# Rotary halves swapped by transfers between SBUF partitions instead of a product with a matrix, in the attention layer and the odd layer

## The chip, the cores and the metric

The kernel runs on one core of a Trainium2 chip. The metric is the device time of one execution in microseconds (us). The core has TensorE for matmuls (PE in the rows, its weight loads PEld), VectorE (DVE), ScalarE (ACT), GpSimd (POOL) and SyncE (SP), and 16 DMA engines; transfers are issued here from the queues of SP and ACT.

## The reference, cut to what matters

Two networks run one behind the other on a sequence of 512 tokens of width 1024: pool, gated delta, latent attention and pool layers, then an even and an odd layer. Two of them rotate queries and keys by position.

```python
# latent attention ("mla"), 16 heads; the last 64 of 192 query channels are rotated, one rotated key for all heads
def rope(x, pos):
    half = x.shape[-1] // 2                      # 32
    inv = ROPE_THETA ** (-jnp.arange(half, dtype=jnp.float32) / half)
    ang = pos.astype(jnp.float32)[..., None, None] * inv
    cos, sin = jnp.cos(ang), jnp.sin(ang)
    x1, x2 = x[..., :half], x[..., half:]
    return jnp.concatenate([x1 * cos - x2 * sin, x1 * sin + x2 * cos], axis=-1).astype(x.dtype)

# odd layer: 8 heads with two maps of 64 channels each; the first 16 of 64 channels are rotated
def partial_rotary(t, pos):
    half = ROT_DIM // 2                          # 8
...
    t1, t2 = tf[..., :half], tf[..., half:ROT_DIM]
    out = jnp.concatenate([t1 * cos - t2 * sin, t2 * cos + t1 * sin, tf[..., ROT_DIM:]], axis=-1)
```

In the odd layer q and k are normalised over their 64 channels (RMS with a gain) before the rotation; in the attention layer the rotated parts are not normalised by themselves. Both layers then do a softmax attention, gate it and project it back onto x.

## The kernel before, in words

Activations lie transposed in SBUF: channels on the 128 partitions, the 512 tokens along the row. All semaphore waits are written out by hand, and each engine runs its own instruction stream in order.

**Weights.** They come from HBM in slots of up to 512 KB into a ring of four (`load_slot`, SP). ACT makes a rounded copy of a slot (`slot_hi`, L276), POOL the remainder in four pieces (`slot_lo`, L291), and `product` multiplies with three matmuls of 512 columns for each block of 128 x 128 (L310, L311, L312) into one of four PSUM banks, `gbank`. PE waits for the remainder and for the bank; the next tile of the bank waits until DVE or ACT has taken the last one. The other four banks, `wbank`, are for everything else.

**Attention layer (`mla_layer`).** A first part (`c_tensor`, `c_vector`, `c_scalar`) projects x onto the latent vectors and the rotary key: eleven slots with one tile each, the fifth the key. Then come 8 pairs of heads. Pair 0's projections run alone (`in_pieces`), and its rotary step after it. Each of seven turns then does, on PE: the attention of pair i (`work_tensor`) with the projections of pair i+1 between its steps, the rest of these, the rotary product (`prep_tensor`, L2325), the output products of pair i (`out_tensor`, two slots with four tiles each). The last pair has no projections beside it. ACT copies the rotary part of q from PSUM into `xr` (`evac_scalar`, L2314, the seventh tile), DVE takes the two gate tiles (`evac_gate`, L2320) and then does the rotary step in `prep_vector`: a product with the cosine (L2334), a product of the rotated tile in PSUM with the sine (L2336), their sum (L2338); then it adds the eight output tiles to x (L482). The next `work_tensor` waits for the sum.

**Odd layer (`odd_layer`).** DVE builds the tables (`tables_vector`, L2592), after it has waited for the norm's factor R; a small matmul of PE (L2616) waits for its step "lq lk", which comes after them. Then 4 pairs of heads in the same manner, with 3 turns. The rotary step has four tiles (two of k, two of q): ACT squares them (L2653), PE sums the squares (`prep_tensor_a`, L2640), ACT makes 1/rms by Ln and Exp (L2656, L2660), DVE multiplies (`prep_vector_a`, L2671), PE multiplies by the rotary matrix (`prep_tensor_b`, L2645), and DVE combines them (`prep_vector_b`, L2679, L2682, L2685). In a turn PE does the sums, one half of the output products (four tiles, `out_half`), the four rotary products, the other half, one projection of the next pair (slot 9), and then the transposes of v (L2695), ahead of which it waits for the last sum of the rotary step. DVE takes the first half's four tiles behind L2671 and one tile of the second half behind each rotary sum, and then the last gate tile (L2633). ACT converts the slots that become free (`hi_after`) between these steps.

**The rotary matrix** is float32, 128 x 128, and each product of 128 x 512 with it goes to the engine as two matmuls. It holds the swap of the halves and the sign.

```python
def prep_tensor(pe, s, i, h):                                                    # L2325
    tp.turn()
    pe.wait_ge(*tile_taken(s, i, *TILES[6]))
    pe.wait_ge(*ve.at("y 1", h, 1))
    pe.matmul(wbank(2), rot, xr, start=True, stop=True).then_inc(*tp.done("rotated"))
```

## Time and profile before

| | us |
|---|---|
| median of 3 runs | 2773.35 |
| lowest, highest | 2770.08, 2773.97 |
| profiled execution, its own time | 2769.89 |
| its span, first to last instruction | 2768.1 |
| mean granted clock of TensorE | 0.976 |

Busy shares of the span: PE 95%, PEld 74%, DVE 58%, POOL 41%, ACT 38%. A busy share is an average over stages; which engine sets the time in a stage is read from the chain of waits and the timelines. Times in a timeline are counted from the span's start. The attention layer runs from about 950 to 1590, the odd layer from about 2375 to the end.

### The profile page before, as it was taken

How to read it: one execution, taken by the hardware profiler on the slowest of the kernel's cores; microseconds unless marked ns; L12 is line 12 of the kernel's file. 1: busy time of each engine (PE TensorE's matmuls, PEld its weight loads, DVE VectorE, ACT ScalarE, POOL GpSimd, SP SyncE). 2: the span in 40 equal slices, each digit the busy share in tenths (PEclk: the TensorE clock that was granted, in tenths of full speed). 3: DMA queues.
4: the chain of work that ended last, by engine and by line, in shares of the span. 5: the costliest groups of instructions: out<-in, count | busy, mean ns of one | idle time of the engine just before them, and what ended most of it. 6: DMA issues, size and time to landing. Idle time of an engine off the chain costs nothing.

```text
span 2768.1 us, 32858 instructions
## 1 busy us (share of the span) xinstructions
PE 2621.5 (95%) x11934; PEld 2042.0 (74%) x11934; DVE 1599.7 (58%) x2703; ACT 1050.3 (38%) x1559; POOL 1141.2 (41%) x1446
## 2 busy tenths in 40 slices
PE   7999998999999898999999899998999998989996
PEld 6888777888888666777777688886887766756664
DVE  4654565777777523444333555556898953366565
ACT  3222343433343433233332422225445663445543
POOL 4666532333333342333333266654554424414320
PEclk9999999999999999999999999999999999999997
DMA  3332311122211221222221233222322212202110
GB/s 122 98 106 92 105 54 39 61 61 62 61 61 46 67 65 54 70 63 70 64 72 54 67 107 99 92 92 77 97 87 69 65 43 76 85 30 69 61 39 31
DMA packets 57106, 196.02 MB, mean 71 GB/s; under 512 B 6416, under 2 KB 8976, under 8 KB 56976
## 3 DMA queue, kind: packets, MB, share of 16 engines
q1 hardware_dynamic: 55824, 192.90, 22.3%
q8 instruction: 82, 1.34, 0.2%
q10 hardware_dynamic: 1152, 1.38, 0.2%
q14 instruction: 48, 0.39, 0.0%
HBM read 192.16 MB, written 2.10 MB: 70 GB/s over the span
## 4 chain that ended last, share of the span: by engine, by line
PE 85%; DVE 9%; ACT 3%; issue 2%; DMA 1%; SPq 0%; ACTq 0%; DVEq 0%
PE psum L310 23%; PE psum L312 22%; PE psum L311 22%; PE psum L1738 3%; PE psum L2393 1%; PE psum L2363 1%; DVE psum L884 1%; PE psum L423 1%; PE psum L1744 1%; PE psum L2366 1%; PE psum L2387 1%; PE psum L2706 1%; PE psum L2735 1%; PE psum L1130 1%; ACT whi L276 1%
## 5 line engine op out<-in xcount | busy, mean ns | idle before, releaser
L291 POOL TENSOR_TENSOR wlo<-raw,whi 128x256 fp32r<-128x256 f32 x1436 | 1140.7, 827 | 1564.9 <-ACT whi L276 1564.9
L310 PE MATMUL psum<-xh,whi 128*128 128x512 f32 x1832 | 763.9, 417 | 15.2 <-DVE xl L404 8.5
L312 PE MATMUL psum<-xh,wlo 128*128 128x512 f32 x1832 | 719.9, 393 | 0.0
L311 PE MATMUL psum<-xl,whi 128*128 128x512 f32 x1832 | 719.1, 393 | 0.0
L276 ACT ACTIVATE whi<-raw 128x1024 fp32r<-128x1024 f32 (+1 forms) x367 | 377.8, 1036 | 803.1 <-PE psum L312 803.1
L310 PEld LDWEIGHTS psum<-xh,whi 128*128 128x128 f32 x1832 | 347.4, 190 | 95.5 <-issue 29.2
L312 PEld LDWEIGHTS psum<-xh,wlo 128*128 128x128 f32 x1832 | 346.5, 189 | 76.2
L311 PEld LDWEIGHTS psum<-xl,whi 128*128 128x128 f32 x1832 | 347.8, 190 | 73.0 <-issue 9.7
L482 DVE TENSOR_TENSOR xT<-psum,xT 128x512 f32<-128x512 f32 x248 | 167.3, 687 | 206.0 <-PE psum L312 206.0
L310 PE MATMUL psum<-pool_yh,whi 128*128 128x512 f32 x256 | 102.5, 400 | 0.0
L311 PE MATMUL psum<-pool_yl,whi 128*128 128x512 f32 x256 | 101.7, 397 | 0.0
L312 PE MATMUL psum<-pool_yh,wlo 128*128 128x512 f32 x256 | 101.5, 396 | 0.0
L576 DVE TENSOR_TENSOR pool_u<-psum,R 128x512 f32<-128x512 f32 x32 | 22.1, 692 | 132.4 <-PE psum L312 132.3
L2323 DVE TENSOR_TENSOR mwork<-psum,R 128x512 f32<-128x512 f32 x16 | 11.1, 691 | 123.1 <-PE psum L312 123.1
L884 DVE SCALAR_TENSOR_TENSOR psum<-e_ue,par,psum 128x512 f32<-128x512 f32 x112 | 79.8, 744 | 0.0
L2435 DVE TENSOR_REDUCE mxs<-psum 128x1 f32<-128x128 f32 (+3 forms) x64 | 31.2, 487 | 77.2 <-PE psum L2368 77.2
L2404 ACT ACTIVATE mwork<-psum,nmx 128x128 f32<-128x128 f32 (+3 forms) x64 | 33.8, 528 | 98.5 <-DVE nmx L2437 98.5
L2318 ACT ACTIVATE mwork<-psum 128x512 f32<-128x512 f32 x48 | 27.6, 596 | 103.1 <-PE psum L312 91.9
L1690 DVE SCALAR_TENSOR_TENSOR g_qv<-pre,par,g_qv 128x512 f32<-128x512 f32 x72 | 64.7, 899 | 1.5
L310 PE MATMUL psum<-cqh,whi 128*128 128x512 f32 x144 | 61.1, 424 | 3.5 <-issue 3.5
L310 PE MATMUL psum<-gyh,whi 128*128 128x512 f32 x128 | 58.9, 460 | 4.4 <-DVE gyl L2022 4.4
L312 PE MATMUL psum<-cqh,wlo 128*128 128x512 f32 x144 | 57.7, 401 | 0.0
(524 smaller groups left out, 4515.4 us busy)
## 6 DMA issues: line engine op xcount, KB each, us to landing
raw<-weights_dram SPq DMA_DIRECT2D x335, 512.0 KB, 3.5
raw<-weights_dram SPq DMA_DIRECT2D x32, 384.0 KB, 3.0
xin<-x_dram SPq DMA_DIRECT2D x4, 512.0 KB, 7.0
out_dram<-y SPq DMA_DIRECT2D x4, 512.0 KB, 2.6
g_masks<-gdn_masks_dram ACTq DMA_DIRECT2D x1, 384.0 KB, 4.1
par<-params_dram SPq DMA_DIRECT2D x1, 326.5 KB, 3.4
mwork<-positions_dram ACTq DMA_DIRECT2D x1, 256.0 KB, 3.0
o_pT<-positions_dram ACTq DMA_DIRECT2D x1, 256.0 KB, 3.1
```

The lines of the kernel that those rows point to most:

```text
L276: act.activation(whi[:, q, 0:nk * nm * P], raw[:, q, 0:nk * nm * P], ACT.Copy).then_inc(hi_ready[q], 1)
L291: last = pool.tensor_tensor(wlo[:, q, part], raw[:, q, part], whi[:, q, part].bitcast(F32), ALU.subtract)
L310: pe.matmul(gbank(b), whi[:, q, c:c + P], h, start=k == 0, stop=False)
L311: pe.matmul(gbank(b), whi[:, q, c:c + P], l, start=False, stop=False)
L312: done = pe.matmul(gbank(b), wlo[:, q, c:c + P], h, start=False, stop=k == nk - 1)
L423: pe.matmul(wbank(0), ones, sq[:, k % 2, :], start=k == 0, stop=k == KD - 1).then_inc(*te.done(f"sum {k}"))
L482: dve.tensor_tensor(xT[:, t, :], tile(sec, j, m), xT[:, t, :], ALU.add).then_inc(*taken(sec, j, m))
L884: dve.scalar_tensor_tensor(out=out, in0=src[:, k:k + SEQ], scalar=w, in1=old, op0=ALU.mult, op1=ALU.add).then_inc(*ve.done(f"tap {c} {k}"))
L1690: dve.scalar_tensor_tensor(out=dst, in0=pre[:, x, k:k + SEQ], scalar=w, in1=dst, op0=ALU.mult, op1=ALU.add).then_inc(*ve.done(f"{i} tap {k ...
L1738: last = pe.matmul(wbank(b)[:, c * P:(c + 1) * P], left[:, c, :], right[:, c, :], start=True, stop=True)
L2404: act.activation(prob[:, hd, off_q[t]:off_q[t] + w], wbank(x % 4)[:, 0:w], ACT.Exp, scale=SCALE, bias=nmx[:, x:x + 1], accum_out=rs[:, x:x ...
L2435: dve.reduce_max(mxs[:, x:x + 1], wbank(x % 4)[:, 0:w], AX.X).then_inc(*ve.done(f"max raw {x}"))
```

## The change

A transfer can move rows to other partitions, so the swap of the halves is left to the DMA engines, and the sign goes into the sine table: the frequencies of the first half of each block are negated on the host, by which the sine changes its sign and the cosine doesn't. In the attention layer ACT issues four transfers of 32 partitions by 512 (64 KB each), for k and after each copy of the rotary part of q, into a new tile `xrot`. In the odd layer ACT issues four transfers of 8 partitions by 2 x 512 (32 KB each) for k once two tiles are normalised, and four for q once all are, into a new tile `rotb`. Its other rows stay zero, for which DVE clears it once, with one instruction at the head of the tables. DVE's sine product now reads these tiles and waits for 64 on the transfers' semaphore. The rotary products, their steps and the matrices are gone.

```diff
@@ attention layer @@
+            def rotate(act, x):
+
+                for r in (0, 64):
+                    act.dma_start(xrot[r:r + 32, :], x[r + 32:r + 64, :]).then_inc(rotated, 16)
+                    act.dma_start(xrot[r + 32:r + 64, :], x[r:r + 32, :]).then_inc(rotated, 16)
...
-                dve.wait_ge(*tb.at("k rotated"))
-                dve.tensor_tensor(krx, wbank(2), sinT[:, :], ALU.mult).then_inc(*vbs.done("k sin"))
+                dve.wait_ge(rotated, 64)
+                dve.tensor_tensor(krx, xrot[:, :], sinT[:, :], ALU.mult).then_inc(*vbs.done("k sin"))
...
                     if j == CKV:
+                        act.wait_ge(*tile_taken(c_sec, 0, CKV, 0))
+                        rotate(act, krx)
                         continue
...
-                    if j == CKV + 2:
-                        pe.wait_ge(*tile_taken(c_sec, 0, CKV, 0))
-                        pe.matmul(wbank(2), rot, krx, start=True, stop=True).then_inc(*tb.done("k rotated"))
...
                 act.activation(dst, tile(s, j, m), ACT.Copy).then_inc(*taken(s, j, m))
+                if t == 6:
+                    act.wait_ge(*tile_taken(s, i, j, m))
+                    rotate(act, xr)
...
-            def prep_tensor(pe, s, i, h):
-                tp.turn()
-                pe.wait_ge(*tile_taken(s, i, *TILES[6]))
-                pe.wait_ge(*ve.at("y 1", h, 1))
-                pe.matmul(wbank(2), rot, xr, start=True, stop=True).then_inc(*tp.done("rotated"))
...
-                dve.wait_ge(*tp.at("rotated", h))
-                dve.tensor_tensor(Rt[:, :], wbank(2), sinT[:, :], ALU.mult).then_inc(*vp.done("sin"))
+                dve.wait_ge(rotated, (h + 2) * 64)
+                dve.tensor_tensor(Rt[:, :], xrot[:, :], sinT[:, :], ALU.mult).then_inc(*vp.done("sin"))
...
@@ odd layer @@
+            rotb = sb("o_rotb", [P, 4, SEQ])
...
             def tables_vector(dve):
+                dve.memset(rotb[:, :, :], 0.0).then_inc(*vbs.done("rotated 0"))
                 dve.wait_ge(pos_in, 32)
...
-            def prep_tensor_b(pe, h):
-                for x in range(4):
-                    pe.wait_ge(*vp.at(f"normed {x}", h))
-                    pe.matmul(wbank(x), rot, xq[:, x, :], start=True, stop=True).then_inc(*tp.done(f"rotated {x}"))
...
                     act.activation(rr[:, x, :], rr[:, x, :], ACT.Exp, scale=-0.5).then_inc(*ap_.done(f"1/rms {x}"))
+                for q in range(2):
+                    act.wait_ge(*vp.at(f"normed {2 * q + 1}", h))
+                    rotate(act, q)
+
+            def rotate(act, q):
+
+                pair = slice(2 * q, 2 * q + 2)
+                for r in (0, 64):
+                    act.dma_start(rotb[r:r + 8, pair, :], xq[r + 8:r + 16, pair, :]).then_inc(rotated[q], 16)
+                    act.dma_start(rotb[r + 8:r + 16, pair, :], xq[r:r + 8, pair, :]).then_inc(rotated[q], 16)
...
-                    dve.wait_ge(*tp.at(f"rotated {x}", h))
+                    dve.wait_ge(rotated[x // 2], (h + 1) * 64)
                     dve.wait_ge(*vp.at(f"cos {x}", h))
-                    dve.tensor_tensor(xq[:, x, :], wbank(x), sinT[:, :], ALU.mult).then_inc(*vp.done(f"sin {x}"))
+                    dve.tensor_tensor(xq[:, x, :], rotb[:, x, :], sinT[:, :], ALU.mult).then_inc(*vp.done(f"sin {x}"))
...
-    out["mla_inv"] = (10000.0 ** (-(r % 32) / 32.0)).astype(np.float32).reshape(P, 1)
+    out["mla_inv"] = (np.where(r % 64 < 32, -1.0, 1.0) * 10000.0 ** (-(r % 32) / 32.0)).astype(np.float32).reshape(P, 1)
```

## Rows read from the trace of the kernel before

**Rows 1.** Page: the chain's shares by engine; one group of DVE.

```profile
PE 85%; DVE 9%; ACT 3%; issue 2%; DMA 1%; SPq 0%; ACTq 0%; DVEq 0%
...
L482 DVE TENSOR_TENSOR xT<-psum,xT 128x512 f32<-128x512 f32 x248 | 167.3, 687 | 206.0 <-PE psum L312 206.0
```

**Rows 2.** Rotary products by line: ns (min, median, max), first and last start.

```profile
L2329 PE MATMUL psum<-sq,mk x16: 590/590/591, 1076.3 to 1522.0; 128*128 128x512 f32 x16
...
L2299 PE MATMUL psum<-mwork,mk x2: 592/592/592, 1007.5 to 1007.9; 128*128 128x512 f32 x2
...
L2645 PE MATMUL psum<-o_xq,o_mk x32: 591/592/1177, 2431.3 to 2685.6; 128*128 128x512 f32 x32
```

**Rows 3.** Timeline, PE at a turn's end: start, length, [idle before <- releaser].

```profile
1521.32 0.39 PE L312 MATMUL psum<-xh,wlo 128*128 128x512 f32 x1
...
1521.55 1.02 PE L2329 MATMUL psum<-sq,mk 128*128 128x512 f32 x2
...
1522.64 0.39 PE L311 MATMUL psum<-myl,whi 128*128 128x512 f32 x1
```

**Rows 4.** The sine product and its addition in the attention layer, by line.

```profile
L2336 DVE TENSOR_TENSOR Rt<-psum,sinT x8: 682/684/685, 1077.7 to 1523.0; 128x512 f32<-128x512 f32 x8
...
L2338 DVE TENSOR_TENSOR mwork<-sq,Rt x8: 693/1212/1217, 1078.4 to 1523.7; 128x512 f32<-128x512 f32 x8
```

**Rows 5.** Timeline: ACT's copy of rotary q; PE behind the first call.

```profile
1510.83 0.60 ACT L2318 ACTIVATE sq<-psum 128x512 f32<-128x512 f32 x1 [2.66 <-PE psum L312]
...
1079.64 1.97 PE L2353 MATMUL psum<-cst,mwork 128*128 128x128 f32 x8 [2.35 <-DVE mwork L2338]
```

**Rows 6.** A memset by line; timelines of DVE and PE at the odd layer's start.

```profile
L569 DVE MEMSET pool_onesrow<- x2: 485/485/485, 38.1 to 1588.1; 128x512 f32 x2
...
2381.18 0.84 DVE L2594 CAST o_maskb<-cst 128x128 bf16<-128x128 f32 x1 [7.09 <-ACT R L440]
...
2386.69 0.38 PE L2616 MATMUL psum<-o_lam,cst 64*128 64x2 f32 x2 [3.48 <-DVE o_lam L2600]
```

**Rows 7.** Timeline of DVE and PE in the first rotary step of the odd layer.

```profile
2430.44 2.74 DVE L2671 SCALAR_TENSOR_TENSOR o_xq<-o_xq,par,o_rr 128x512 f32<-128x512 f32 x4 [8.21 <-ACT o_rr L2660]
...
2434.01 0.69 DVE L2682 TENSOR_TENSOR o_xq<-psum,o_sinT 128x512 f32<-128x512 f32 x1
...
2441.86 1.97 PE L2695 MATMUL psum<-cst,o_vT 128*128 128x128 f32 x8 [5.21 <-DVE o_qr L2685]
```

**Rows 8.** Timeline: an ACT issue. Two groups of issues (KB, us to landing).

```profile
2375.22 0.46 ACTq L2901 DMA_DIRECT2D o_mk<-odd_masks_dram  x1
...
pool_head<-pool_head_dram ACTq DMA_DIRECT2D x2, 32.0 KB, 1.9
...
xin<-x_dram SPq DMA_DIRECT2D x4, 512.0 KB, 7.0
```

**Rows 9.** Timelines of PE, DVE and POOL in the first odd turn.

```profile
2514.03 3.60 PE L2645 MATMUL psum<-o_xq,o_mk 128*128 128x512 f32 x8
...
2528.53 1.04 PE L2695 MATMUL psum<-cst,o_vT 128*128 128x128 f32 x8
...
2514.79 2.48 DVE L482 TENSOR_TENSOR xT<-psum,xT 128x512 f32<-128x512 f32 x4
...
2517.19 0.83 DVE L2679 TENSOR_TENSOR o_rr<-o_xq,o_cosT 128x512 f32<-128x512 f32 x1
...
2526.73 1.09 DVE L2685 TENSOR_TENSOR o_qr<-o_rr,o_xq 128x512 f32<-128x512 f32 x1
...
2515.37 3.25 POOL L291 TENSOR_TENSOR wlo<-raw,whi 128x256 fp32r<-128x256 f32 x4 [5.10 <-ACT whi L276]
```

**Rows 10.** Timeline: PE's sums, first odd turn; DVE's gate copy, third.

```profile
2504.91 3.70 PE L2640 MATMUL psum<-o_rr,o_mk 128*128 128x512 f32 x8 [1.67 <-ACT o_rr L2653]
...
2697.30 0.69 DVE L2633 TENSOR_TENSOR o_gs<-psum,R 128x512 f32<-128x512 f32 x1 [0.63 <-PE psum L312]
```

**Rows 11.** Stretch: us, busy time by engine, granted clock (PEclk), DMA share, GB/s.

```profile
2442.00:2446.00 4.00, 3.22 (x13) 2.49 (x14) 1.29 (x2) 0.00 (x0) 0.00 (x0) 0.50 0.00 0
```

More of the change, by code:

```diff
@@ L2173, in mla_layer @@
             kr = sb("kr", [P, SEQ])
-            mk = sb("mk", [P, 2, P])
-            rot = mk[:, 0, :]
+            mk = sb("mk", [P, P])
+            xrot = sb("mla_xrot", [P, SEQ])
             maskb = sb("maskb", [P, 2, P], BF16)
@@ L2217, in c_vector @@
                 dve.tensor_copy(identb, ident).then_inc(*vbs.done("identity"))
-                dve.tensor_copy(causal, mk[:, 1, :]).then_inc(*vbs.done("mask"))
+                dve.tensor_copy(causal, mk[:, :]).then_inc(*vbs.done("mask"))
                 rotary_tables(dve, None, vbs, ab, "vector", pos_i, cosT[:, :], sinT[:, :], tmp, param("mla_inv"),
@@ L2532, in tables @@
                 act.dma_start(pos_i, T["positions"].to_broadcast([P, SEQ])).then_inc(pos_in, 16)
-                act.dma_start(mk[:, :, :], T["mla_masks"].rearrange("p (k n) -> p k n", k=2)).then_inc(pos_in, 16)
+                act.dma_start(mk[:, :], T["mla_masks"]).then_inc(pos_in, 16)
             def sync(sp):
@@ L2558, in odd_layer @@
             sinT = sb("o_sinT", [P, SEQ])
-            mk = sb("o_mk", [P, 3, P])
-            rot, halves = mk[:, 0, :], mk[:, 2, :]
+            mk = sb("o_mk", [P, 2, P])
+            halves = mk[:, 1, :]
+            rotb = sb("o_rotb", [P, 4, SEQ])
             maskb = sb("o_maskb", [P, 2, P], BF16)
@@ L2580, in odd_layer @@
             tmp = [rr[:, 0, :], rr[:, 1, :], rr[:, 2, :]]
-            pos_in = sem("odd_pos_in")
+            pos_in, rotated = sem("odd_pos_in"), [sem(f"odd_rotated_{name}") for name in ("k", "q")]
             wq, wk, subln = param("c_q_norm_w"), param("c_k_norm_w"), param("c_subln_w")
@@ L2592, in tables_vector @@
             def tables_vector(dve):
+                dve.memset(rotb[:, :, :], 0.0).then_inc(*vbs.done("rotated 0"))
                 dve.wait_ge(pos_in, 32)
                 dve.tensor_copy(identb, ident).then_inc(*vbs.done("identity"))
-                dve.tensor_copy(allowed, mk[:, 1, :]).then_inc(*vbs.done("mask"))
+                dve.tensor_copy(allowed, mk[:, 0, :]).then_inc(*vbs.done("mask"))
                 rotary_tables(dve, None, vbs, ab, "vector", pos_i, cosT[:, :], sinT[:, :], tmp, param("odd_inv"),
@@ L3131, in small_parameters @@
     r = np.arange(P)
-    out["mla_inv"] = (10000.0 ** (-(r % 32) / 32.0)).astype(np.float32).reshape(P, 1)
+    out["mla_inv"] = (np.where(r % 64 < 32, -1.0, 1.0) * 10000.0 ** (-(r % 32) / 32.0)).astype(np.float32).reshape(P, 1)
     out["c_norm_w"] = columns(A["c_norm_w_2"][0])
-    out["odd_inv"] = np.where(r % 64 < 16, 500000.0 ** (-2.0 * (r % 8) / 16.0), 0.0).astype(np.float32).reshape(P, 1)
+    out["odd_inv"] = np.where(r % 64 < 16, np.where(r % 64 < 8, -1.0, 1.0) * 500000.0 ** (-2.0 * (r % 8) / 16.0),
+                              0.0).astype(np.float32).reshape(P, 1)
     for name in ("c_q_norm_w", "c_k_norm_w"):
@@ L3183, in constants @@
         c[f"join {s}"] = (p // (2 * s) == x // (2 * s)) & (p // s % 2 == 0) & (x // s % 2 == 1)
-    rot = np.zeros((P, P), np.float32)
-    for m in range(P):
-        if m % 64 < 32:
-            rot[m + 32, m] = -1.0
-        else:
-            rot[m - 32, m] = 1.0
-    orot = np.zeros((P, P), np.float32)
-    for m in range(P):
-        if m % 64 < 8:
-            orot[m + 8, m] = -1.0
-        elif m % 64 < 16:
-            orot[m - 8, m] = 1.0
     t = np.arange(SEQ)
     head = np.stack([w * (1.0 / np.minimum(t + 1, w)).astype(np.float32) for w in WINDOWS])[:, 0:PAD].astype(np.float32)
-    odd_masks = [orot, np.where((x >= 64) & (p < 64), NEG, 0.0), p // 64 == x // 64]
+    odd_masks = [np.where((x >= 64) & (p < 64), NEG, 0.0), p // 64 == x // 64]
     return {"odd_masks": np.concatenate([m.astype(np.float32) for m in odd_masks], axis=1),
-            "mla_masks": np.concatenate([rot, np.where(x > p, NEG, 0.0).astype(np.float32)], axis=1),
+            "mla_masks": np.where(x > p, NEG, 0.0).astype(np.float32),
             "consts": np.concatenate([c[k].astype(np.float32) for k in ("identity", "ones")], axis=1),
```

12 lines of the change are left out of this document (4 added, 8 removed).

## The prediction

> **What bounds the kernel now.** I read the chain of work that ended last first: 85% of it is TensorE (PE), 9% VectorE (DVE) [rows 1]. The costliest groups say the same from the other side: DVE's additions of a product to x sat idle 206 us, all of it waiting for a product of PE [rows 1]. So in a stretch where PE has no idle time, a PE instruction taken away is gained, and DVE work added there is free. The timelines of the two layers then show where this does not hold: the start of the odd layer, the first rotary step of each layer, and the end of each odd turn, where DVE is as long as PE.
>
> **What is removed from PE.** A rotary product is one call and two matmuls of 590 to 592 ns in the trace (their spans overlap; what counts is how much later the next one starts). There are 8 calls in the attention turns, 1 for k, 16 in the odd layer [rows 2].
> - Attention turns: at the end of a turn L312 starts at 1521.32, and after the rotary product L311 of the next product starts at 1522.64. Neighbours start 0.23 apart, so without it L311 would start at 1521.78: 0.86 us [rows 3]. PE is busy on both sides and then goes into eight output products, in which DVE waits. 7 of the 8 calls stand so: 7 x 0.86 = -6.0 us. What takes their place is hidden: ScalarE (ACT) copies the rotary part of q out at 1510.83 and DVE's sine product starts at 1523.0, 12 us later [rows 4, 5]; four transfers of 64 KB issued by ACT need some 4 us of it (below). ACT issues them ahead of a conversion of weights, which comes some 1.8 us later; PE needs that slot only after two more products of 24 matmuls at 0.23 (11 us), so nothing is late.
> - k: a product of the same length [rows 2] among the first projections, PE busy around it, and what follows (the norms of c, DVE's operands) hangs on PE's last product: -0.86 us. DVE asks for its swap only after four more projections of 24 matmuls, 22 us.
> - The first attention call: PE waits for DVE behind it (2.35 us idle [rows 5]), so its removal is worth 0.
> - The odd layer: below, since the gain there depends on DVE.
>
> **What the sine product costs DVE.** It read PSUM and now reads two SBUF tensors. In the attention turns the PSUM form took 682 to 685 ns every time, also beside GpSimd (POOL); the addition behind it, with two SBUF inputs, took 693 ns alone but 1212 at the median, that is 0.52 us more, and in the odd turn 1.09 [rows 4, 9]. I read this as DVE waiting for a running POOL instruction, between 0 and 0.52 us a time, and take 0.45 for each one that meets POOL. The Trainium skill has this as a rule that speaks against this change: in "SBUF — State Buffer", section "🔬 SBUF: two separate sides", a DVE instruction with two SBUF inputs and a GpSimd instruction exclude each other for a whole instruction. These rows agree with it for the addition; for the sine product no row of before shows it. A second rule of the Trainium skill, in "VectorE: DVE Perf Modes", section "⚠️ The TRN2 errata — SBUF-src ops pay a fixed extra latency per instruction", has a PSUM source cost 62 cycles more than an SBUF one, about 65 ns as an estimate, which would give back 0.26 us in an odd turn. The trace disagrees: the PSUM form is not the longer one (684 against 693 ns alone) [rows 4].
> - In attention turns this is covered: DVE has 0.7 us idle ahead of nearly every addition to x, and it catches up. In the first call DVE's chain is what PE waits for, one hit more: +0.5 (0 to 0.8).
>
> **The start of the odd layer.** DVE now clears four 512-column tiles, after its wait for R and ahead of the tables [rows 6]. A memset of 512 columns took 485 ns, so 4 x 0.485 = 1.94 us. PE already waits 3.48 us there, for DVE's lambda step, which comes after the tables; nothing covers the memset. The CAST at 2381.18 took 0.84 us beside POOL and may get shorter behind the memset, by less than its length. So +1.1 to +1.94; I take +1.5.
>
> **The first rotary step of the odd layer.** Here the chain is ACT, DVE, PE; POOL is idle. The four normed tiles start at 2430.44, two of them are done by 2431.9; the sine product started at 2434.01, and PE waited 5.21 us for the end of it [rows 7]. Afterwards ACT issues four transfers from 2431.9. An issue took 0.46 us, a transfer of 32 KB landed 1.9 us after its issue, the heaviest 7.0 [rows 8]. The fourth is issued at about 2433.3 and lands at about 2435.2: +1.4 us (0.5 to 3; SBUF to SBUF is in no row, the nearest is the small one of 32 KB). The second pair has 3 us more. PE's rotary products lay in its idle time: 0.
>
> **The three odd turns.** PE starts the rotary products at 2514.03; they hold it for 8 x 0.43 = 3.44 us, to 2517.47. Without them the next output half has to wait for a bank: the same four banks hold the first half, and DVE takes them only behind its normed tiles, from 2514.79, first done at 2515.48 [rows 9]. PE starts at 2515.5, so it is 2.0 us ahead, and would be ready for the transposes at 2526.55 in place of 2528.53. But those wait for the last rotary addition, which ends at 2527.8. So even with no cost at all only 0.7 of 3.44 us is left, and 0.5 behind it, since DVE must still copy the gate. Two normed tiles are done at 2513.6, so the swap lands by 2517.0, before the cosine product ends at 2518.0 [rows 9]: no wait there.
>
> Now the four sine products. Two batches of POOL (8 instructions) run in DVE's rotary stretch, the first at 2515.37 [rows 9]; eight issues of ACT push it to about 2518. DVE's cosine, sine and addition then all have two SBUF inputs, each waits for the one before, and POOL slips in between. Followed with 0.6 and 0.7 us a piece, sine products and additions meet POOL six times: 6 x 0.45 = 2.7, where before it was 0.15 for the first cosine product (0.83) and 0.40 for the last addition (1.09) [rows 9]. The last addition ends 2.15 us later, at 2529.95. PE is 1.4 us later than before, and it has been idle for 3.4 us. After an idle of 2.35 us the eight transposes took 1.97 us, against 1.04 in the turn, and behind the idle of 5.21 the granted clock was 0.50, the level of 1.2 GHz, for the 4 us from 2442 [rows 5, 7, 9, 11]. Transposes slower by 0.93 and a clock at half for some 5 us cost about 2.4 us. So +3.8 us each in the first two turns. In the third POOL has nothing to do, and the gate's copy, before which DVE was idle 0.63 us, is earlier by that: -0.6 [rows 10]. Together +7.0.
>
> **The sum.** -6.0 - 0.86 + 0.5 + 1.5 + 1.4 + 7.0 = +3.5 us. The profiled execution took 2769.89 us (span 2768.1), so it becomes 2773.4. That execution is the fastest of four (2769.89, 2770.08, 2773.35, 2773.97); their middle is 2771.7, the median of the runs 2773.35. I forecast 2775, the sum laid on the middle of the four, rounded. A measurement of this kernel can tell about 0.2%, 5.5 us, from no change.
>
> **The rivals.**
> - The sine products don't meet POOL (the form of the instruction matters less than I think). Then the first call costs 0, the turns give -0.5 - 0.5 - 0.6: -6.0 - 0.86 + 1.5 + 1.4 - 1.6 = -5.6, some 2766. For it: a cosine product with two SBUF inputs beside POOL is not always longer. Against it: the additions.
> - They meet POOL, but PE's clock holds over the idle of 3.4 us, or the idle is shorter: 3.5 - 4.8 = -1.3, some 2770.5. The rows of 2.35 and 5.21 us speak against it.
> - Slower than before: the transfers land late. A load of weights may be under way beside them, and their rows lie in few partitions. The place is the first sine product of each odd step. The first step has no reserve, so each us of landing beyond 1.9 costs one; in the turns the reserve is 1.0 us, from there each us costs one three times. At the landing of 7.0 us: first step +5 more, the turns 3 x 3.9, about a third of which falls together with waits for POOL: +3.5 + 5 + 8 = +16, some 2788. It decides from a landing of about 3.5 us. For it stands only the row of 7.0, of four transfers of 512 KB at once; against it the small ones.
> - The clock also falls after the bank wait of 1.45 us: 3 x 2.4 more, +10.7, some 2782. Against it: in the same turns PE is idle 1.67 us ahead of the sums of squares, and those eight matmuls then take no longer than 0.46 us each, 3.70 in all [rows 10].
>
> **How the numbers follow.** Forecast 0.42, no meeting 0.23, clock holds 0.17, late landing 0.08, clock at the bank wait 0.05, other 0.05. The range reaches from the first rival with its scatter to the forecast with the upper ends of its terms: 2765 to 2781. Faster by over 0.2%: half of the first rival and a little of the second, 0.15. Slower: a quarter of the forecast's cases, late landing and the clock, 0.22. Within: 0.63.
>
> **What would show it.** In the attention turns L311 follows L312 with no gap and each turn is 0.86 us shorter. In the odd turns PE shows a wait of about 1.4 us for DVE's addition to x, then one of 3 us for the last rotary addition, with transposes of 1.97 us in two turns of three; sine products of 1.1 to 1.2 us beside POOL. At the odd layer's start PE waits about 5 us for lambda. The sine product of the first odd step starts about 3.5 us behind the second normed tile. If the sine products stay at 0.68 us the term of 7.0 is wrong; if the transfers take over 3.5 us the sign of the whole is.

## The result, and the profile after

The kernel after took 2779.71 us at the median (2776.86 to 2781.78, 15 runs), the kernel before, timed beside it, 2774.39 us (2769.94 to 2777.51, 15 runs). The ratio is 1.0022, 95% interval 1.0015 to 1.0029: slower by some 5.3 us. The forecast was 2775, with a sum of +3.5 and a range of 2765 to 2781; I held a change within 0.2% for the likeliest, and the ratio lies just outside, with that bound inside its interval. The profiled execution of after took 2781.18 us, its span is 2779.4.

The page of after answers to [rows 1]: the chain of work that ended last, and DVE's additions to x.

```profile
PE 83%; DVE 10%; ACT 4%; issue 3%; DMA 1%; ACTq 0%; SPq 0%; DVEq 0%
...
L482 DVE TENSOR_TENSOR xT<-psum,xT 128x512 f32<-128x512 f32 x248 | 166.6, 687 | 197.8 <-PE psum L312 197.8
```

Two points of the chain's share went from PE to DVE, ACT and issue. To see where, I put the two traces side by side at the same instructions. The table has the times between two instructions in the one profiled execution of each kernel, in us.

| stretch | before | after | difference | in the sum |
|---|---|---|---|---|
| DVE's first CAST of the attention layer to the first transposes of a pair | 115.43 | 116.38 | +0.95 | -0.36 |
| to the transposes of the eighth pair (seven turns) | 453.96 | 447.82 | -6.14 | -6.0 |
| to lambda's matmul at the odd layer's start | 853.09 | 853.58 | +0.49 | +1.5 |
| to the first normed tile | 43.75 | 44.77 | +1.02 | 0 |
| to the first transposes (first rotary step) | 11.42 | 14.25 | +2.83 | +1.4 |
| to the normed tiles of the first turn | 70.28 | 70.90 | +0.62 | 0 |
| first to second turn's normed tiles | 84.30 | 88.30 | +4.00 | +3.8 |
| second to third | 84.20 | 88.41 | +4.21 | +3.8 |
| third to the end of the span | 87.46 | 87.07 | -0.39 | -0.6 |

These add up to +7.6, 2.3 more than the medians differ. Ahead of the first row, where no instruction differs, the profiled execution of after is 3.7 us late; over the twelve profiles of this study that first CAST comes at 963.0 to 968.6. The profiled execution of before (2769.89) is also 4.5 us below the median of its runs. Stretches without a changed instruction differ by up to 1.3 us from kernel to kernel (see the last section); the -1.0 that is left of the third row beside the memset's +1.47 (below) is of that kind. So a total of one execution is worth little here. A stage of some 10 to 90 us is worth more, above all where several kernels repeat it.

**Attention layer.** Timeline of after where it was 1521.32 to 1522.64 in [rows 3], of the first rotary step ([rows 5]), and the sine product by line ([rows 4]; the first numbers are ns, min/median/max):

```profile
1520.69 0.39 PE L312 MATMUL psum<-xh,wlo 128*128 128x512 f32 x1
1520.92 0.40 PE L310 MATMUL psum<-myh,whi 128*128 128x512 f32 x1
...
1081.89 1.22 DVE L2337 TENSOR_TENSOR Rt<-mla_xrot,sinT 128x512 f32<-128x512 f32 x1
1083.14 1.10 DVE L2339 TENSOR_TENSOR mwork<-sq,Rt 128x512 f32<-128x512 f32 x1
...
1084.30 1.97 PE L2354 MATMUL psum<-cst,mwork 128*128 128x128 f32 x8 [3.65 <-DVE mwork L2339]
...
L2337 DVE TENSOR_TENSOR Rt<-mla_xrot,sinT x8: 685/1231/1232, 1081.9 to 1522.3; 128x512 f32<-128x512 f32 x8
```

The output products follow at 0.23 with no gap, and a turn is 0.88 us shorter (6.14 / 7). The sine product takes 1.23 us at the median instead of 0.68, and it costs something only in the first step, where PE waits for DVE's chain in both kernels.

**Start of the odd layer and first rotary step** ([rows 6, 7]). DVE, ACT's queue and PE:

```profile
2379.19 1.76 DVE L2593 MEMSET o_rotb<- 128x2048 f32 x1 [7.55 <-ACT R L440]
2380.87 0.16 DVE L2595 CAST o_maskb<-cst 128x128 bf16<-128x128 f32 x1
...
2385.70 0.58 PE L2617 MATMUL psum<-o_lam,cst 64*128 64x2 f32 x2 [4.95 <-DVE o_lam L2599]
...
2431.91 1.21 ACTq L2665 DMA_DIRECT2D o_rotb<-o_xq  x1
2433.16 0.65 ACTq L2666 DMA_DIRECT2D o_rotb<-o_xq  x1
...
2434.50 0.63 ACTq L2666 DMA_DIRECT2D o_rotb<-o_xq  x1
...
2436.88 0.69 DVE L2688 TENSOR_TENSOR o_xq<-o_rotb,o_sinT 128x512 f32<-128x512 f32 x1 [2.95 <-DMA o_rotb<-o_xq]
```

The memset takes 1.76 us, but the CAST behind it only 0.16 in place of 0.84: from the start of this work of DVE to lambda's matmul it is 6.51 us, before 5.51. That is not all of it. ACT finishes R at 2378.70 and the memset starts 0.49 us later, where the CAST of before started 0.03 behind R. From the end of R to lambda's matmul it is 7.00 us, before 5.54, and PE waits 4.95 in place of 3.48: the memset costs 1.47. The four issues last from 2431.91 to 2435.13, 0.63 us each and 1.21 for the first, and DVE waits 2.95 us for the landing.

**First odd turn** ([rows 9]): DVE's rotary pieces, POOL, PE.

```profile
2521.58 0.69 DVE L2688 TENSOR_TENSOR o_xq<-o_rotb,o_sinT 128x512 f32<-128x512 f32 x1 [0.23 <-DMA o_rotb<-o_xq]
...
2524.24 1.11 DVE L2688 TENSOR_TENSOR o_xq<-o_rotb,o_sinT 128x512 f32<-128x512 f32 x1
2525.38 1.12 DVE L2691 TENSOR_TENSOR o_kn<-o_rr,o_xq 128x512 f32<-128x512 f32 x1
2526.42 0.68 DVE L482 TENSOR_TENSOR xT<-psum,xT 128x512 f32<-128x512 f32 x1
...
2523.84 9.07 POOL L291 TENSOR_TENSOR wlo<-raw,whi 128x256 fp32r<-128x256 f32 x8 [10.10 <-ACT whi L276]
...
2519.07 0.47 PE L310 MATMUL psum<-o_yh,whi 128*128 128x512 f32 x1 [1.40 <-issue]
...
2533.51 1.09 PE L2701 MATMUL psum<-cst,o_vT 128*128 128x128 f32 x8 [3.14 <-DVE o_qr L2691]
...
2535.38 1.39 PE L2712 MATMUL psum<-o_kn,o_qr 64*128 64x128 f32 x4 [0.79 <-DVE o_vt L2779]
```

While POOL runs, sine products and their additions take 1.11 us (six pieces in this turn); the addition to x, with one operand in PSUM, stays at 0.68 in the same microseconds. ACT's eight issues keep its conversions back, so POOL's two batches come together, as eight instructions in 9.07 us, 5.0 us later against the normed tiles than before. PE waits 3.14 us for the last rotary addition; the transposes behind it still take 1.09, the score products 1.39 in place of 1.08: there the clock falls. Stretches of after and of before behind it (us, busy time by engine, PEclk, DMA share, GB/s):

```profile
2537.00:2541.00 4.00, 4.00 (x11) 3.14 (x11) 1.70 (x6) 2.73 (x6) 4.00 (x7) 0.50 0.15 18
```

```profile
2532.00:2536.00 4.00, 4.00 (x21) 2.82 (x20) 2.05 (x8) 2.54 (x7) 4.00 (x7) 1.00 0.17 16
```

Eleven matmuls instead of 21 in 4 us: 0.50 is the level of 1.2 GHz. In the third turn POOL has nothing to do, all pieces take 0.69, and PE waits 0.74:

```profile
2706.34 0.69 DVE L2688 TENSOR_TENSOR o_xq<-o_rotb,o_sinT 128x512 f32<-128x512 f32 x1
...
2707.81 1.09 PE L2701 MATMUL psum<-cst,o_vT 128*128 128x128 f32 x8 [0.74 <-DVE o_qr L2691]
```

### The profile page after: what moved, and what is told of

The parts are those of the page before. It is cut to its first block, busy times and chain, and to the rows that moved or that the text cites. A ratio compares the mean times of both kernels' runs of the same rounds, so it can differ in the third digit from the quotient of the medians.

```text
span 2779.4 us, 32801 instructions
## 1 busy us (share of the span) xinstructions
PE 2608.6 (94%) x11884; PEld 2039.6 (73%) x11884; DVE 1607.4 (58%) x2704; ACT 1051.1 (38%) x1559; POOL 1146.3 (41%) x1446
## 4 chain that ended last, share of the span: by engine, by line
PE 83%; DVE 10%; ACT 4%; issue 3%; DMA 1%; ACTq 0%; SPq 0%; DVEq 0%
PE psum L310 22%; PE psum L311 21%; PE psum L312 21%; PE psum L1738 3%; PE psum L2394 1%; PE psum L2364 1%; DVE psum L884 1%; PE psum L423 1%; PE psum L1744 1%; PE psum L2367 1%; PE psum L2712 1%; DVE xT L482 1%; PE psum L2388 1%; PE psum L2741 1%; PE psum L1130 1%
## 5 line engine op out<-in xcount | busy, mean ns | idle before, releaser
L276 ACT ACTIVATE whi<-raw 128x1024 fp32r<-128x1024 f32 (+1 forms) x367 | 377.9, 1036 | 793.7 <-PE psum L312 762.0
L311 PE MATMUL psum<-cql,whi 128*128 128x512 f32 x144 | 58.2, 404 | 0.0
```

The source lines that it names most:

```text
L276: act.activation(whi[:, q, 0:nk * nm * P], raw[:, q, 0:nk * nm * P], ACT.Copy).then_inc(hi_ready[q], 1)
L311: pe.matmul(gbank(b), whi[:, q, c:c + P], l, start=False, stop=False)
```

## The experiments

My theory was: the attention half is a gain; in the odd layer the form of the sine products (two SBUF inputs) makes DVE wait for POOL, PE becomes idle ahead of the transposes and loses its clock; issues, landing and the memset add to it at the layer's start. Rivals: the transfers and issues cost the turns; the clock falls for another reason; the number of DVE's instructions is what costs, not their form.

### Each half alone

The attention layer and its table from after, the odd layer from before, here in words and not in code:

```diff
-    odd_layer as after
+    odd_layer as before, and its rotary matrix
```

> The transfers in the attention layer alone; the odd layer as before. The removed rotary products should be worth 7 x 0.86 + 0.86 = 6.9 us, less 0.5 us for the first step and up to 1 us for the clock behind it: 5.4 to 6.9 us faster than before, ratio 0.9975 to 0.998. If instead the transfers themselves cost time wherever they run (traffic, ACT's issues), it gains less than 3 us, ratio above 0.999.

Measured: 2766.58 us (2765.45 to 2769.39, 9 runs) against 2773.96 (25 runs), ratio 0.9975 [0.9965, 0.9985]: 7.4 us faster. Seven turns took 447.78 us, as in after, and the odd layer's first step and turn are those of before (11.41 and 84.28 us). The second turn took 85.12, before 84.20, with nothing changed in it. PE waits 1.82 us there ahead of the sums of squares that belong to the third turn's rotary step, in this kernel and in before:

```profile
2670.96 5.37 PE L2639 MATMUL psum<-o_rr,o_mk 128*128 128x512 f32 x8 [1.82 <-ACT o_rr L2652]
...
2673.51 3.67 PE L2640 MATMUL psum<-o_rr,o_mk 128*128 128x512 f32 x8 [1.82 <-ACT o_rr L2653]
```

The first line is of this kernel, the second of before. The wait is the same, but here the granted clock behind it falls to 0.50 (it is 0.50 from 2671.2 to 2674.5), and in before and the ten other profiles of this study it stays at 1.00. The repeat of this same kernel, below, took 84.19 us for that turn.

The other half, the attention layer from before and the odd layer from after, again in words:

```diff
-    mla_layer as after
+    mla_layer as before, and its rotary matrix
```

> The transfers in the odd layer alone; the attention layer as before. By stages of the two traces the odd layer lost 13.3 us: 1 for the memset, 1 for the clock behind it, 2.8 and 0.6 for the first step, 4.0 and 4.2 in two turns, -0.4 in the third. So 10 to 14 us slower than before, ratio 1.0037 to 1.005. If the difference of the two kernels came mostly from the attention layer or from drift, it is slower by under 6 us.

Measured: 2786.93 us (2783.54 to 2791.08, 5 runs), ratio 1.0047 [1.0033, 1.0061]: 13.0 us slower. First step 14.31, turns 88.31 and 88.38 us. PE ahead of the transposes of the first turn:

```profile
2541.05 1.09 PE L2702 MATMUL psum<-cst,o_vT 128*128 128x128 f32 x8 [3.15 <-DVE o_qr L2692]
```

The halves are -7.4 and +13.0, together +5.6, and the whole was +5.3: they add. The change is a gain in one layer and a loss in the other.

### The odd layer without its transfers

This kernel leaves out the swapped half of the rotation in the odd layer: ACT issues no transfer, and the sine product reads the cleared tile. Every instruction of DVE keeps its form.

```diff
@@ prep_scalar @@
-                for q in range(2):
-                    act.wait_ge(*vp.at(f"normed {2 * q + 1}", h))
-                    rotate(act, q)
@@ prep_vector_b @@
-                    dve.wait_ge(rotated[x // 2], (h + 1) * 64)
```

> The changed kernel without the transfers in the odd layer: ACT issues none, DVE's sine product reads the cleared tile and waits only for the cosine product. Left out is the swapped half of the rotation in the odd layer; the attention layer is as in the changed kernel. All instruction forms of DVE stay. My theory (the form of the sine product, two SBUF inputs beside POOL, costs the turns; the transfers cost only the first step): from the first normed tile to the transposes 11.4 us in the first step, as before (14.25 in the changed kernel), but from turn to turn still 87 to 88.3 us (88.30 and 88.41 in the changed kernel, 84.30 and 84.20 before), transposes 3 us late behind an idle PE, the clock down behind them. Total about 2776 us. Rival (the issues on ACT and the waits for the transfers cost the turns): turns of 84.3 to 85 us, total about 2769 us.

Measured: 2773.83 us (2771.86 to 2774.67, 10 runs), ratio 0.9992 [0.9982, 1.0002]. The first step took 11.13 us, the turns 87.63 and 86.19, the second of them shorter than the 87 to 88.3 that I expected; the total is 2.2 us under the expected 2776. First turn, DVE, POOL and PE, and the stretch behind it:

```profile
2518.72 1.11 DVE L2677 TENSOR_TENSOR o_xq<-o_rotb,o_sinT 128x512 f32<-128x512 f32 x1
...
2521.80 0.69 DVE L2677 TENSOR_TENSOR o_xq<-o_rotb,o_sinT 128x512 f32<-128x512 f32 x1
...
2516.01 3.28 POOL L291 TENSOR_TENSOR wlo<-raw,whi 128x256 fp32r<-128x256 f32 x4 [5.11 <-ACT whi L276]
2523.30 4.18 POOL L291 TENSOR_TENSOR wlo<-raw,whi 128x256 fp32r<-128x256 f32 x4 [4.01 <-ACT whi L276]
...
2529.58 1.09 PE L2690 MATMUL psum<-cst,o_vT 128*128 128x128 f32 x8 [2.07 <-DVE o_qr L2680]
...
2533.00:2537.00 4.00, 4.00 (x12) 3.14 (x11) 1.69 (x6) 2.80 (x6) 4.00 (x7) 0.50 0.02 6
```

No transfer and no issue is left, and the first turn is still 3.3 us over before: POOL's two batches are apart again, DVE meets them in three long pieces and two of 0.85 in place of six long ones, PE waits 2.07 us in place of 3.14, and the clock falls all the same. In the second turn PE waits 2.08 us again, but the low clock is shorter: the pair's second score product starts 7.50 us behind the transposes in place of 8.75. So without any transfer 5.3 of the 8.2 us of the two turns are still there (3.3 of 4.0, and 2.0 of 4.2). Most of these 5.3 us is the clock: the transposes are only 0.4 us later against the normed tiles than before, where in after they are 1.5 later. The issues account for the other 1.1, since they push POOL's batches together, so that DVE meets POOL in more pieces. The two causes act together: this run shows what the transfers add to the form, the next ones what is left when the form is changed and the transfers stay. In the first step it is the other way round: all of its +2.8 is the transfers.

### Sine table in PSUM, then all tables and sums in PSUM

What makes DVE wait is taken away without taking POOL away. First the sine table is copied into a bank that is free between the sums and the transposes, and the cosine products are written to the three others:

```diff
@@ prep_vector_a @@
+                dve.wait_ge(*ap_.at("ln 3", h))
+                dve.tensor_copy(wbank(0), sinT[:, :]).then_inc(*vp.done("sine in psum"))
@@ prep_vector_b @@
-                    dve.tensor_tensor(rr[:, x, :], xq[:, x, :], cosT[:, :], ALU.mult)
+                    c = wbank(1 + x % 3)
+                    dve.tensor_tensor(c, xq[:, x, :], cosT[:, :], ALU.mult)
...
-                    dve.tensor_tensor(xq[:, x, :], rotb[:, x, :], sinT[:, :], ALU.mult)
+                    dve.tensor_tensor(xq[:, x, :], rotb[:, x, :], wbank(0), ALU.mult)
...
-                    dve.tensor_tensor(dst, rr[:, x, :], xq[:, x, :], ALU.add)
+                    dve.tensor_tensor(dst, c, xq[:, x, :], ALU.add)
```

> The changed kernel, but in the odd layer's rotary step the sine table is copied to a PSUM bank once a step (in DVE's idle time) and the cosine products are written to PSUM, so that the sine product and the addition have one SBUF input each. If these wait for GpSimd because of their two SBUF inputs, they take 0.69 us in all turns, the last addition of turns 1 and 2 ends about 2.9 us sooner, PE's idle time before the transposes falls from 3.1 to under 0.5 us, the clock stays up, and each of the two turns gets about 4 us shorter: some 8 us less than the changed kernel. If the transfers are what delays DVE, nothing changes.

Measured: 2775.39 us (2773.11 to 2777.24, 10 runs), ratio 1.0004 [0.9995, 1.0014], turns of 86.09 and 87.13 us. First turn, DVE and PE:

```profile
2524.56 1.28 DVE L2688 TENSOR_TENSOR psum<-o_xq,o_cosT 128x512 f32<-128x512 f32 x1
2525.87 0.69 DVE L2691 TENSOR_TENSOR o_xq<-o_rotb,psum 128x512 f32<-128x512 f32 x1
...
2530.58 1.09 PE L2704 MATMUL psum<-cst,o_vT 128*128 128x128 f32 x8 [1.83 <-DVE o_qr L2694]
```

Sine products and additions are now at 0.69 beside POOL. But the cosine product, which still reads two SBUF tensors, takes 1.28 us twice; in after it took 0.67 to 0.69 in the same place. The difference lies in what POOL was doing. The first two lines are the third cosine product of after and a piece of POOL, the last a piece of POOL in this run:

```profile
2527.02 0.68 DVE L2685 TENSOR_TENSOR o_rr<-o_xq,o_cosT 128x512 f32<-128x512 f32 x1
2527.06 1.23 POOL L291 TENSOR_TENSOR wlo<-raw,whi 128x256 fp32r<-128x256 f32 x1
...
2524.55 0.73 POOL L291 TENSOR_TENSOR wlo<-raw,whi 128x256 fp32r<-128x256 f32 x1
```

In after DVE starts 0.04 us ahead of POOL's piece, and that piece becomes long; here POOL's piece starts 0.01 us ahead of the cosine product, and DVE waits for all of it. So more than half of PE's wait stays (1.83 of 3.14 us), the clock falls in both turns, and the run gained about half of the 8 us that I expected. The second kernel copies the cosine table into a bank as well:

```diff
+                dve.tensor_copy(wbank(1), cosT[:, :]).then_inc(*vp.done("cosine in psum"))
...
-                    c = wbank(1 + x % 3)
-                    dve.tensor_tensor(c, xq[:, x, :], cosT[:, :], ALU.mult)
+                    c = wbank(2 + x % 2)
+                    dve.tensor_tensor(c, xq[:, x, :], wbank(1), ALU.mult)
```

> As the run with the sine table in PSUM, and now the cosine table is copied into a second bank too, and the cosine products go to the two that are left: none of DVE's twelve rotary instructions in an odd step has two SBUF inputs. My theory (DVE waits for POOL only with two SBUF inputs, and PE's clock falls because PE is idle for that): every cosine, sine and addition 0.69 us in all turns, also beside POOL; PE idle ahead of the transposes 1.0 us or less; turns of 84.3 to 85.3 us in place of 86.1 and 87.1 with the sine table alone and 88.3 in the changed kernel. The copies are two of 0.7 us; the second may hold up the first normed tile by 0.6 us in the first step. Total about 2772 us. Rival A (what costs is the number of operations of DVE in the turn, whatever their form): turns stay at 86 to 87 us. Rival B (the clock falls for the wait for a bank at the output half, and not for the wait ahead of the transposes): DVE's pieces are at 0.69, but the turns stay at about 86 us with the clock down.

Measured: 2769.3 us (2766.71 to 2771.23, 10 runs), ratio 0.9981 [0.9971, 0.999]. Turns of 83.32 and 83.15 us. First turn, DVE beside POOL, PE, and the stretch behind it:

```profile
2525.87 0.68 DVE L2689 TENSOR_TENSOR psum<-o_xq,psum 128x512 f32<-128x512 f32 x1
2526.59 0.69 DVE L2692 TENSOR_TENSOR o_xq<-o_rotb,psum 128x512 f32<-128x512 f32 x1
2527.31 0.69 DVE L2695 TENSOR_TENSOR o_qr<-psum,o_xq 128x512 f32<-128x512 f32 x1
...
2523.55 5.62 POOL L291 TENSOR_TENSOR wlo<-raw,whi 128x256 fp32r<-128x256 f32 x8 [10.10 <-ACT whi L276]
...
2530.70 1.09 PE L2705 MATMUL psum<-cst,o_vT 128*128 128x128 f32 x8 [0.63 <-DVE o_qr L2695]
...
2534.00:2538.00 4.00, 4.00 (x21) 2.85 (x20) 2.00 (x8) 2.91 (x6) 4.00 (x6) 1.00 0.03 4
```

All pieces take 0.69 beside POOL, POOL's eight need 5.62 us in place of 9.07, PE waits 0.63, and the clock stays at 2.4 GHz. The turns are 1.0 us shorter than before the change, although DVE does two copies more; I had expected 84.3 to 85.3. The number of DVE's instructions falls as a rival, and so does the wait for a bank: that is still there (1.39 us), and the clock holds. The Trainium skill says, in "SBUF — State Buffer", section "🔬 SBUF: two separate sides", that DVE with two SBUF inputs and GpSimd exclude each other; by that rule the trace agrees, on both sides: DVE's 1.11 and POOL's 9.07 us become 0.69 and 5.62 together, and in the rows above the one that starts second is the one that becomes long.

### PE kept busy ahead of the transposes

All of DVE's waits stay; PE only gets three products of constants to do while it would wait; nothing reads their results.

```diff
@@ turn, after the projection of slot 9 @@
+                    pe.wait_ge(*ap_.at("ln 3", i + 1))
+                    for _ in range(3):
+                        pe.matmul(wbank(3), halves, cosT[:, :], start=True, stop=True)
```

> The changed kernel with three products of a constant (128 x 128 by 128 x 512, results never read) on PE ahead of the transposes in each odd turn, 2.6 us of work in the idle time of 3.1 us. If 2.4 us a turn are lost to the lower clock behind that idle time, the transposes start as late as in the changed kernel but run on at full clock, and turns 1 and 2 get 2 to 2.5 us shorter each, the third up to 2 us longer: 2 to 5 us less in all. If the clock has no part, the kernel is 2 us slower than the changed one (third turn) and the stretch behind the transposes is as long as there.

Measured: 2774.96 us (2773.3 to 2777.03, 10 runs), ratio 1.0007 [0.9997, 1.0016]; turns of 85.82 and 85.72 us. PE in the first turn, and the stretch behind it:

```profile
2527.67 2.74 PE L2861 MATMUL psum<-o_cosT,o_mk 128*128 128x512 f32 x6
2530.97 1.09 PE L2701 MATMUL psum<-cst,o_vT 128*128 128x128 f32 x8 [0.56 <-DVE o_qr L2691]
...
2536.88 0.70 PE L2712 MATMUL psum<-o_kn,o_qr 64*128 64x256 f32 x4
...
2534.00:2538.00 4.00, 4.00 (x22) 2.85 (x21) 1.90 (x7) 3.19 (x7) 3.78 (x6) 1.00 0.00 0
```

From the transposes to the next pair's second score product it is 5.91 us; before 5.88 (2528.53 to 2534.41), in after 8.39 (2533.51 to 2541.90). The transposes are as late as in after (17.88 us behind the first normed tile, 17.89 there), yet the turn is 2.5 and 2.7 us shorter: that is the part of the 4 us that the clock takes, and DVE's lateness is the other 1.5.

### The memset ahead of DVE's wait for R

```diff
@@ norm of x, DVE @@
+                for f in ahead_of_r:
+                    f(dve)
                 dve.wait_ge(*ae.of("R"))
@@ tables_vector @@
-                dve.memset(rotb[:, :, :], 0.0).then_inc(*vbs.done("rotated 0"))
```

> The changed kernel with the clearing of the odd layer's tile moved ahead of DVE's wait for R, where DVE is idle for 7.5 us. My theory: lambda's matmul comes 1.0 us earlier (from the attention layer's CAST to it 1416.8 us in place of 1417.8) and PE's idle time ahead of it is 4.0 in place of 4.95; the longer low clock behind it, 1.0 us, goes too, so that from lambda's matmul to the first normed tile it is 43.8 us as before and not 44.8. Total 2.0 us less, about 2777.7 us. Rival (the low clock behind lambda comes from elsewhere): only the 1.0 of the memset, about 2778.7 us; a second rival, that the clearing only shifts the wait to something else that DVE does: 0.

Measured: 2775.93 us (2773.03 to 2778.9, 10 runs), ratio 1.0007 [0.9997, 1.0016]: 1.0 us above the kernel before in the same rounds, where after was 5.3 above it in its own. That is 4.3 us less than after, where I had expected 2.0. DVE and PE:

```profile
2369.56 1.76 DVE L2920 MEMSET o_rotb<- 128x2048 f32 x1 [0.38 <-issue]
...
2376.27 0.84 DVE L2597 CAST o_maskb<-cst 128x128 bf16<-128x128 f32 x1 [4.95 <-ACT R L440]
...
2381.79 0.50 PE L2619 MATMUL psum<-o_lam,cst 64*128 64x2 f32 x2 [3.49 <-DVE o_lam L2601]
```

The CAST is back at 0.84 us and PE's wait at 3.49 (before 3.48, and 4.0 expected), from the end of R to lambda's matmul it is 5.55 us as before, and from lambda to the first normed tile 43.74, as before. The granted clock of the 10 us from lambda's matmul on is 0.83 here and in before, and 0.72 in after. So the memset costs twice: 1.47 us directly and 1.0 us of low clock behind the longer wait. In the profile that is 2.5 us from the first CAST of the attention layer to the first normed tile (1460.06 in place of 1462.55); the rest of the gain lies in stretches in which no instruction differs.

### What the parts give together

Tables and sums in PSUM with the early memset; the two diffs above, nothing else.

> The run with both tables and the sums in PSUM and the run with the clearing ahead of R put together. My theory (the two costs are apart): from the attention layer's CAST to the first normed tile 2.4 us less than in the changed kernel, as in the run with the early clearing (1460.1 in place of 1462.6), and turns of 83.3 us, as with the tables in PSUM. Total 2 us under the 2769.3 of the latter, about 2767.3 us. Rival (the granted clock has a budget that one idle time less only moves to another place): one of the two gains is missing, 2769 us.

Measured: 2768.75 us (2766.66 to 2770.33, 10 runs), ratio 0.9981 [0.9971, 0.999]. That is 0.55 us under the one without the early memset, where 2 were expected, and the kernel before was 0.55 us faster in these rounds too (2774.41 against 2774.96): the ratio is the same, and the gain is missing. From the first CAST to the first normed tile it took 1460.12 us, as expected, but the first turn took 84.86, with the second at 83.21. PE in the first turn, and the stretch behind it:

```profile
2527.68 1.09 PE L2707 MATMUL psum<-cst,o_vT 128*128 128x128 f32 x8 [0.60 <-DVE o_qr L2697]
...
2531.00:2535.00 4.00, 4.00 (x12) 2.97 (x11) 1.53 (x6) 2.89 (x6) 4.00 (x6) 0.61 0.02 8
```

The wait is 0.60 us, not longer than the 0.63 of the run in which the clock held, and here it fell. The transposes stand 3 us earlier in the execution; I see no other difference in that turn that would explain it. So a short wait doesn't exclude the low clock. The total is what my rival gave, one of the two gains missing (2769 us), and one profile of each kernel can't say whether the clock's low time moves from one place to another or falls by chance.

Last, the first rotary step by products with a matrix of zeros and ones, where nothing stands beside it, and transfers in the three turns alone. In the first step the sine product reads the product in PSUM again, and the copies of the tables shrink to one column. Cut to what matters:

```diff
@@ before the loop of the turns, PE @@
+                for x in range(4):
+                    pe.wait_ge(*vp.at(f"normed {x}", 0))
+                    pe.matmul(wbank(x), swap, xq[:, x, :], start=True, stop=True).then_inc(swapped, 1)
@@ prep_scalar @@
-                for q in range(2):
+                for q in range(0 if isinstance(h, int) and h == 0 else 2):
```

> As the run before it, but the first rotary step of the odd layer, in which nothing stands beside it, takes its swap from products with a matrix of zeros and ones, and only the three turns use the transfers. My theory (in the first step the transfers only add their issues and their landing, 2.8 us): from the first normed tile to the transposes 11.4 us in place of 14.3, turns of 83.3 us. Total about 2764.5 us, 2 us under the kernel with transfers in the attention layer alone. Rival (PE's shorter idle time there gives nothing, since the low clock behind it is what counts): 12.5 us or more and a total of about 2766 us.

Measured: 2765.9 us (2764.48 to 2767.89, 11 runs), ratio 0.9971 [0.9962, 0.998]. PE in the first step:

```profile
2426.45 5.39 PE L2864 MATMUL psum<-o_xq,o_mk 128*128 128x512 f32 x8 [4.26 <-DVE o_xq L2684]
...
2437.05 1.97 PE L2714 MATMUL psum<-cst,o_vT 128*128 128x128 f32 x8 [5.21 <-DVE o_qr L2704]
```

The step is 11.41 us, as before, and the total is 2.9 us less than with transfers there (2768.75). The first turn took 86.84 us, with the clock down behind a wait of 1.19 us, the second 83.21. The longer wait has a cause: the first issue of these transfers, 1.21 us in after, now stands in the first turn and takes 1.22 there, and DVE's sine product waits 0.78 us for the landing. I had expected 2764.5, and 2 us less than the kernel with transfers in the attention layer alone. That kernel was timed beside it:

> The kernel with transfers in the attention layer alone once more, beside the run before it, so that the two are timed on the same chip in the same rounds. Expected 2766.6 us as before, that is 2 us above the one with the first step by product. If the gain of the odd turns is not real the two are equal.

Measured: 2767.05 us (2762.42 to 2769.23, 9 runs), ratio 0.9974 [0.9964, 0.9984]. The two differ by 1.2 us, and their intervals overlap: they can't be told apart. The simple kernel, transfers only in the attention layer, is the version I would keep: 7.4 us faster than before in both series, and some 13 us faster than after.

## Why the prediction was right or wrong

The sign and the size of the sum held (+3.5 against +5.3), the time lay in the range, and near its upper end. The mechanism of the two largest terms, the attention turns and the first two odd turns, was right. That the total came within 1.8 us of the sum is in part luck: the changed stages of the profile add up to +7.6, the sum had +3.5 for them, and nothing in the trace explains why the medians differ by 2.3 less. Point by point:

- **Attention turns, -6.0: right** (-6.14). The cover held too: no wait for a transfer shows in them, though 64 KB took 3.4 us at the median to land.
- **First part and first call, -0.36: +0.95 in the profile.** The rotary product of k gave its 0.86 (from 982 to 1036 us) and the sine product cost its 0.5. What the sum didn't have is that the low clock behind PE's wait of 3.52 us at 1054 lasted 1.1 us longer. No changed instruction stands there, the wait itself is the same in both kernels, and no run took this apart.
- **Memset, +1.5: +1.47, plus 1.0 that was missing.** "Nothing covers the memset" was right. The memset was shorter than 1.94 (1.76), the CAST got shorter by 0.68, and the memset began 0.46 us later behind R than the CAST had, which the sum didn't have; that these come to the forecast is luck in the parts. What I failed to price is the clock behind a longer wait, which I had priced in the turns. The run with the early memset shows both.
- **First odd step, +1.4 (0.5 to 3): +2.8.** The mechanism was right and the size was not. Term by term: the fourth issue started at 2434.50 and not at 2433.3, since an issue of these transfers takes 0.63 us and the first 1.21, where I took 0.46 from a load from HBM; from its start to DVE's sine product it was 2.4 us in place of 1.9.
- **First two odd turns, +3.8 each: +4.0 and +4.2.** The six meetings are there (+0.42 each by the rows), the last addition ends 2.16 us later behind the first normed tile (2.15 forecast), PE's transposes start 1.5 us later (1.4), PE's wait is 3.14 (3.4), and the clock takes 2.5 in the first turn and 2.7 in the second (2.4). One detail was wrong: the transposes themselves kept the high clock (1.09 us, not 1.97), and the clock fell some 2 us later, during the score products. The run with a busy PE separates the two terms, and the one with everything in PSUM shows that both are gone when no piece of DVE has two SBUF inputs. That the clock would fall was a fair forecast and not a certain one: behind shorter waits it held in one kernel and fell in another.
- **Third turn, -0.6: -0.4.** Right, and for the reason given: no POOL, no meeting.
- **POOL's batches.** I had POOL pushed to about 2518, 2.6 us later; it was pushed by 5.0, and the two batches became one. Without issues the first turn is 0.7 us shorter and the second 2.2, so this belongs to the price of the transfers, not only to that of the form.

Of the rivals, "sine products don't meet POOL" fell by the rows of 1.11 us; "the clock holds" fell by the granted clock of 0.50; "late landing" was half right in its place, the first step, and wrong in the turns, where DVE waited 0.23 and 0.20 us; "the clock also falls after the bank wait" fell, since it held there (1.40 us of wait, with the following output products at 0.39).

What stays open: the attention half alone gave 7.4 us, in two series, where its stages of the profile show some 5 to 6; the rest is within what unchanged stretches differ by. It is also open what decides whether the clock falls behind a wait of a given length.

## What to carry to other kernels

Ask of each operand that moves from PSUM to SBUF what runs on GpSimd at that moment: a chain of DVE instructions with two SBUF inputs, each waiting for the last, lost 0.42 us a piece here. With one table and the cosine products in PSUM the first two turns got back 3.5 of the 8.2 us that they had lost; with both tables in PSUM they got back all of it and 2.0 us more. A transfer in place of a product pays where ACT and DVE have slack (attention turns: 12 us), and not where the chain ACT, DVE, PE is the critical one, because a group of four issues alone takes 2.7 us, and 3.2 with the first issue of its kind in it. When a sum makes PE wait longer anywhere, price the low clock behind the wait too: it cost 1.0 us at the memset, beside 1.5 of its own, and 2.5 and 2.7 us in the two turns, beside 1.5.

## What the runs showed of the hardware

- A swap issued from ACT's queue takes 0.63 us of the queue for each transfer of 32 KB between SBUF partitions (1.21 for the first one of the kernel, 1.22 where that first one came a turn later), against 0.46 for a load from HBM [rows 8].
- How long a DVE piece with two SBUF inputs takes beside POOL follows from what is left of the POOL piece that runs when it starts. In the odd steps of before, after and the six runs that keep DVE's forms or those of before, it took 1.08 to 1.12 us with 0.53 to 0.57 left, 0.83 to 0.86 with 0.27 to 0.31 left, and 0.67 to 0.68 with 0.07 or 0.08 left: what is left and some 0.55 more. The cosine products of 1.27 to 1.28 us had nearly all of a piece of 0.73 ahead of them, and their PSUM output did not free them.
- A memset of 2048 columns took 1.76 us and started 0.49 us behind R in each of the six profiles that have it there; the CAST in its place started 0.03 behind R in the other six.
- Whether the clock falls is not settled by the length of the wait alone. At the same place of the first odd turn it held behind 0.56 and 0.63 us, and fell behind 0.60, 1.19, 1.83, 2.07 and 3.14 us; in the second turn it held behind 0.57 to 0.61 in all four kernels with such a wait. Ahead of the sums of squares for the third turn's rotary step it held behind 1.82 us in eleven profiles and fell in one.
- Stretches without a changed instruction came in steps. From the eighth pair's transposes to lambda's matmul, less the memset's 1.47 us where it is there, it is 852.1 to 852.2 us in seven profiles, 853.4 to 853.5 in four, and 853.1 in before; the seven attention turns by transfer took 447.8 or 447.9 in seven profiles and 448.9 or 449.0 in three. One execution can't settle a microsecond here.
